# Forget-gate logits: 16 wide products with stacked weight parts, and a small product that adds the halves

## What is computed

```python
h = rmsnorm(x, norm_g[l])
proj = h @ w_in[l]
(cv_a, cv_b, cv_gate, fq, fk, fv, f_logit, fox_gate, mq, mem_gate) = jnp.split(proj, SPLITS, axis=-1)
...
logf = jax.nn.log_sigmoid(f_logit.astype(jnp.float32) + b_f[l].astype(jnp.float32))
...
cT = jnp.cumsum(logf, axis=1)
bias = ci[..., :, None] - cT[..., None, :]
```

## Time and profile before

| | us |
|---|---|
| median of 3 runs | 1780.23 (1780.03 to 1782.44) |
| the profiled execution | 1780.92 |
| its span (first to last instruction) | 1779.1 |
| PE busy | 1759.7 (99%) |
| DVE busy | 1257.5 (71%) |
| ACT busy | 942.1 (53%) |

### The profile page before, as it was taken

One profiled execution on the slowest core, in us unless ns is written; L12 is line 12 of the kernel. 1 busy time (PEld: TensorE's weight loads), 2 busy tenths in 40 slices (PEclk: granted clock), 3 DMA queues, 4 the chain that ended last, 5 costly groups with the idle time before them and its releaser, 6 DMA issues.

```text
span 1779.1 us, 29674 instructions
## 1 busy us (share of the span) xinstructions
PE 1759.7 (99%) x10231; PEld 1545.9 (87%) x10231; DVE 1257.5 (71%) x1590; ACT 942.1 (53%) x1254; POOL 616.6 (35%) x621
## 2 busy tenths in 40 slices
PE   9999999999999999999999999999999999999997
PEld 7888888888888888888888888888888888888886
DVE  6877777765598777777777644445887688887754
ACT  5544554544476555555555533334655566775532
POOL 1743345556703333111111422221252255550032
PEclk9999999999999999999999999999999999999999
DMA  8444444436565555555555555556455444444453
GB/s 315 174 160 168 167 167 176 166 142 237 189 237 189 189 189 189 189 189 189 189 189 189 168 194 184 189 194 208 166 189 201 166 166 165 165 166 165 166 189 118
DMA packets 51008, 326.61 MB, mean 184 GB/s; under 512 B 5776, under 2 KB 6416, under 8 KB 18320
## 3 DMA queue, kind: packets, MB, share of 16 engines
q1 hardware_dynamic: 49808, 323.86, 51.1%
q10 hardware_dynamic: 1152, 2.11, 0.3%
HBM read 323.85 MB, written 2.10 MB: 183 GB/s over the span
## 4 chain that ended last, share of the span: by engine, by line
PE 93%; DVE 3%; ACT 2%; DMA 1%; issue 1%; ACTq 0%; DVEq 0%; SPq 0%
PE ps L1803 57%; PE ps L1804 29%; DVE wlo L971 1%; ACT whi L466 1%; PE ps_sc L1842 1%; PE ps_lev L1928 1%; PE ps_t L1832 1%; PE ps_lev L1878 1%; DMA x_in<-in_x_turned 0%; PE ps_lev L1803 0%; DMA stage<-in_w_a 0%; PE bank_b L1933 0%; DMA stage<-in_w_b 0%; PE bank_a L1847 0%; DVE big L1408 0%
## 5 line engine op out<-in xcount | busy, mean ns | idle before, releaser
L1803 PE MATMUL ps<-act_a,whi 128*128 128x512 f32 x3056 | 1069.2, 394 | 0.0
L971 DVE TENSOR_TENSOR wlo<-stage,whi 128x2048 fp32r<-128x2048 f32 (+1 forms) x315 | 695.1, 2207 | 250.5 <-ACT whi L466 245.7
L1804 PE MATMUL ps<-act_a,wlo 128*128 128x256 f32 x3056 | 854.3, 280 | 0.0
L1803 PEld LDWEIGHTS ps<-act_a,whi 128*128 128x128 f32 x3056 | 573.7, 188 | 125.3 <-issue 0.5
L466 ACT ACTIVATE whi<-stage 128x2048 fp32r<-128x2048 f32 (+1 forms) x315 | 567.7, 1802 | 126.2 <-DMA stage<-in_w_down 103.6
L1804 PEld LDWEIGHTS ps<-act_a,wlo 128*128 128x128 f32 x3056 | 574.0, 188 | 0.3
L1803 PE MATMUL ps<-big,whi 128*128 128x512 f32 x1568 | 546.3, 393 | 3.5 <-DVE big L1408 1.3
L1804 PE MATMUL ps<-big,wlo 128*128 128x256 f32 x1568 | 438.3, 280 | 0.0
L473 ACT ACTIVATE small<-ps 128x256 f32<-128x256 f32 x242 | 92.7, 383 | 534.1 <-PE ps L1804 534.1
L1803 PEld LDWEIGHTS ps<-big,whi 128*128 128x128 f32 x1568 | 294.4, 188 | 70.1 <-DVE wlo L971 2.4
L1804 PEld LDWEIGHTS ps<-big,wlo 128*128 128x128 f32 x1568 | 294.3, 188 | 0.1
(11 more groups left out here) (373 smaller groups left out, 1340.2 us busy)
## 6 DMA issues: line engine op xcount, KB each, us to landing
stage<-in_w_a SPq DMA_DIRECT2D x166, 1024.0 KB, 4.8
stage<-in_w_b SPq DMA_DIRECT2D x87, 1024.0 KB, 4.8
stage<-in_w_down SPq DMA_DIRECT2D x64, 704.0 KB, 4.0
stage<-in_w_a SPq DMA_DIRECT2D x8, 256.0 KB, 8.6
mem_raw<-in_memT SPq DMA_DIRECT2D x1, 2048.0 KB, 9.6
mem_again<-in_memT SPq DMA_DIRECT2D x1, 2048.0 KB, 9.2
x_in<-in_x_turned ACTq DMA_DIRECT2D x7, 256.0 KB, 9.3
x_in<-in_xT SPq DMA_DIRECT2D x3, 512.0 KB, 8.9
```

Source lines behind the costliest of these rows:

```text
L971: dve.tensor_tensor(wlo[:, slot, part], stage[:, slot, part], whi[:, slot, part].bitcast(F32), ALU.subtract).then_inc(w_lo, 1)
L1803: pe.matmul(dst, whi[:, slot, c * P:(c + 1) * P], act, start=start, stop=False)
L1804: return pe.matmul(dst[:, T:2 * T], wlo[:, slot, c * P:(c + 1) * P], act[:, 0:T], start=False, stop=stop)
```

## The change

1. `wfg_hi` and `wfg_lo` become the left and right 48 columns of one tile `wfg_parts` (2048 x 96). ACT and DVE write the same numbers as before, each to its half of the columns. The tile lies elsewhere in the work area.
2. On PE, 48 products of 256 columns (3 for each of 16 feature tiles) become 16 of 512 columns with 96 stationary columns. They stand behind block 5 instead of behind block 7.
3. The result has 96 rows x 512 columns: rows of the high weight part over rows of the low part, and the activation's high part left of its low part. DVE adds the column halves (a copy from PSUM, then an add) behind `add(6)` in the conv stage's last step. It also builds `both_rows` (96 x 48, two identities over each other).
4. Behind block 7, PE waits for these (`fl_added`) and adds the row halves with one product in plain fp32, 96 rows x 256 columns, with `both_rows` as its stationary operand. That product now signals `fl_ready`. (The product of the two low parts, left out before, is in the sum now.)

```diff
-        wfg_lo = over("wfg_lo", big_at, w2[0], [P, KT, FOX_ROWS], F32R)
...
-        wfg_hi = over("wfg_hi", big_at, w2[0], [P, KT, FOX_ROWS], F32R)
+        wfg_parts = over("wfg_parts", big_at, w2[0], [P, KT, 2 * FOX_ROWS], F32R)
+        wfg_hi, wfg_lo = wfg_parts[:, :, 0:FOX_ROWS], wfg_parts[:, :, FOX_ROWS:2 * FOX_ROWS]
...
+        both_rows = work2("both_rows", [2 * FOX_ROWS, FOX_ROWS])
...
+            rows = slice(0, 2 * FOX_ROWS)
             for n in range(GROUPS):
                 u = U_CONV + 2 * n
                 add(u, 0)
+                if n == GROUPS - 1:
+                    dve.wait_ge(s("fl_parts"), 1)
+                    link(dve.tensor_tensor(both_rows[:, :], ident[rows, 0:FOX_ROWS], ident[rows, FOX_ROWS:2 * FOX_ROWS], ALU.add))
+                    link(dve.tensor_copy(fs[rows, T:2 * T], ps_t[rows, T:2 * T]))
+                    dve.tensor_tensor(fs[rows, 0:T], ps_t[rows, 0:T], fs[rows, T:2 * T], ALU.add).then_inc(s("fl_added"), 1)
...
             for j in range(2, 2 * GROUPS):
                 whole(G_CONV, 0, 0, j, U_CONV + j, j % 2, act_a)
-            pe.wait_ge(*event("wfg_ready"))
-            logits = ps_t[0:FOX_ROWS, 0:T]
-            for k in range(KT):
-                pe.matmul(logits, wfg_hi[:, k, :], act_a[:, k, 0:T], start=k == 0, stop=False)
-                pe.matmul(logits, wfg_hi[:, k, :], act_a[:, k, T:2 * T], start=False, stop=False)
-                ins = pe.matmul(logits, wfg_lo[:, k, :], act_a[:, k, 0:T], start=False, stop=k == KT - 1)
-            ins.then_inc(s("fl_ready"), 1)
+                if j == 2 * GROUPS - 3:
+                    pe.wait_ge(*event("wfg_ready"))
+                    for k in range(KT):
+                        ins = pe.matmul(ps_t[0:2 * FOX_ROWS, :], wfg_parts[:, k, :], act_a[:, k, :], start=k == 0, stop=k == KT - 1)
+                    ins.then_inc(s("fl_parts"), 1)
+            pe.wait_ge(s("fl_added"), 1)
+            pe.matmul(ps_t[0:FOX_ROWS, 0:T], both_rows[:, :], fs[0:2 * FOX_ROWS, 0:T], start=True, stop=True).then_inc(s("fl_ready"), 1)
```

More of the change, by code:

```diff
@@ L824, in _ @@
                     act.wait_ge(s("fox_in"), 3 * 16)
-                    act.activation(wfg_hi[:, :, :], wfg[:, :, :], ACT.Copy).then_inc(event("wfg_split")[0], 1)
+                    act.activation(wfg_hi, wfg[:, :, :], ACT.Copy).then_inc(event("wfg_split")[0], 1)
             act.wait_ge(*event("z_abs"))
@@ L1478, in _ @@
                     dve.wait_ge(*event("wfg_split"))
-                    dve.tensor_tensor(wfg_lo[:, :, :], wfg[:, :, :], wfg_hi[:, :, :].bitcast(F32),
+                    dve.tensor_tensor(wfg_lo, wfg[:, :, :], wfg_hi.bitcast(F32),
                                       ALU.subtract).then_inc(event("wfg_ready")[0], 1)
```

## The result

| | us |
|---|---|
| the changed kernel, median of 9 runs | 1786.56 (1784.99 to 1787.81) |
| the kernel before, median of 9 runs beside it | 1781.03 (1779.84 to 1782.44) |
| ratio, 95% interval | 1.0031 (1.0023 to 1.0040) |
| the profiled execution of the changed kernel | 1787.81, span 1786.0 |

The change makes the kernel slower, by 5.5 us (4.1 to 7.1 by the interval). The forecast was 1783.5, with a range up to 1785.5: the direction holds, the size doesn't. The profiled execution is the slowest of the nine, so lengths read from its trace lie on the long side.

The account below looks back on a forecast made before the run. PE was taken to bound the kernel, with no reserve towards DVE at block 11. From 1780.23, +1.9 (list -1.27, wait +3.3, existing loss -0.14) and +1.4 for the clock gave 1783.5 us, range 1780.6 to 1785.5.

Parts of the forecast that it names:

- PE's list: PE's own work: 5.61 us of old logits products replaced by 3.70 wide and 0.64 small, 1.27 us shorter.
- wait at block 11: PE reaches block 11 at T + 17.29 but may start only at T + 20.55, so it waits 3.3 us.
- clock: PE's clock falls to half in the wait, block 11 begins at half rate: +1.4 us, bounds 0 and 5.55.
- T: The moment when block 7 is through on PE, from which the prediction counts; 3.70 us later in the changed kernel.
- PE has no reserve at block 11: Block 11 needs DVE's `add(9)` and already lost 0.14 us; PE arriving earlier without an earlier `add(9)` must wait.
- `zf`, exp and ln holding `evac(8)`: `zf` stays at T + 5.87; `evac(8)` queues behind ACT's exp and ln until about T + 9.6.
- DVE's three instructions hidden: Between `add(6)` and `lo(9)`, DVE's new instructions take 1.0 us, covered by 1.38 us of idle time.
- no wait: Rival: PE doesn't wait at block 11 and keeps its 1.27 us, giving 1779.0 us; chance 0.06.
- Slower by over 0.2%: Rival: clock stays low through block 11's first half or longer, costing 2.8 us, total 1784.9; chance 0.23.
- the term for POOL: POOL's taps lengthening DVE's instructions before `add(9)`: bounds -0.87 (no hit) and +0.87 (a second one), taken as 0.
- the prediction's bound for one hit: By the strict port rule, a DVE instruction could lose a whole POOL instruction at once, 2.96 us.
- the chain from T to `evac(8)`: From block 7's end through `zf`, exp and ln, ACT frees `evac(8)` at about T + 9.6, 1.76 sooner than before.

Follow-up runs that it names:

- pool_late: The changed kernel with POOL's first convolution taps held until DVE has made `cpos` and `cneg`; 1782.44 us, 1.0010 against the kernel before.
- moved_only: The kernel before with its 48 old logits products only moved from behind block 7 to behind block 5; 1788.25 us, ratio 1.0045 against the kernel before.
- act_first: The changed kernel with ACT's `evac(8)` and `hi(11)` moved ahead of the forget gate's exp and ln; 1779.89 us, 0.9994 against the kernel before.
- act_first_pool_late: The changed kernel with ACT's `evac(8)` and `hi(11)` ahead of exp and ln, and POOL's first taps held until `cpos` and `cneg`; 1779.20 us, ratio 0.9993.
- keep_clock: The changed kernel with 18 small dummy products on PE between block 10 and block 11; 1785.11 us, 1.0021 against the kernel before.

## Why the prediction was wrong

Per term, from the changed kernel's trace:

| term | forecast | measured |
|---|---|---|
| wide products | 3.70 | 3.74 |
| small product | 0.64 | 0.76 |
| PE's list | -1.27 | -1.11 |
| wait at block 11 | +3.3, less the 0.14 of before | +5.6, less 0.05 |
| clock | +1.4 | +1.6 |
| sum | +3.3 | +6.06 |

Measured: the small product's 0.76 is the second pair of block 8 (1396.74) less T less a pair's 0.35; it includes 0.1 more than the column sums, which I leave unexplained. The wait is block 11's start, 1418.65, less what PE alone would make, T + 0.76 + 16.65 = 1413.04; the 0.05 is how late block 11 started before. The clock's term is 7.33 - 5.73 (before: 1418.76 - 1413.03). Of the 2.3 by which the wait is longer than forecast, POOL makes 2.04 and the later `evac(8)` 0.45, less 0.12 for the dearer small product.

Part of the miss in the median, 3.06 us, isn't the change's: the sum starts from 1780.23, the median of three runs, and the nine runs beside the changed kernel have 1781.03. That is 0.8.

**What held.** The reading that PE has no reserve at block 11; `zf`, exp and ln holding `evac(8)`; DVE's three instructions hidden; the wait there, put down to DVE; the clock falling in it, in all nine executions as their mean clocks say (0.996 or 0.997, against 0.998 in the execution before). The "no wait" rival is out by the trace. "Slower by over 0.2%" came true (5.5 us against 3.56), but not by a clock that stays low: that needed over 1.66 us, and the clock cost 1.6. A further hit by POOL, which it named only beside that, is what decided.

**What failed: the term for POOL.** I bounded it by -0.87 and +0.87 and took 0. It measured +2.04 (10.22 against 8.18). I had seen one of DVE's instructions hit beside POOL's first add and allowed one more like it. I had not worked out which instructions would lie beside which of POOL's adds. The trace of before had all that was needed. ACT waited there for PE twice, 1.75 us ahead of `evac(8)` and 1.39 us ahead of `evac(9)`:

```profile
1407.63 0.38 ACT L473 ACTIVATE small<-ps 128x256 f32<-128x256 f32 x1 [1.39 <-PE ps L1804]
```

In the sum I used the first of these waits only. The second goes too, and with it ACT's products for POOL, and POOL's adds, come 1.5 us earlier against the gate: from the start of `lo(11)` to POOL's first add it was 1410.68 - 1404.30 = 6.38 us, now it is 1412.77 - 1407.88 = 4.89. So the gate's last instructions run into three adds and not one. Three of these records are longer than before: 0.89 (1.24 - 0.35), 0.90 (1.89 - 0.99), and 0.24 for `cpos` (1.51 - 1.27, it was hit before too). That makes 2.03. pool_late showed it by taking all of it away.

The rule of the Trainium skill that I weighed and left at the edge ("SBUF — State Buffer", the section on the two separate sides: a lock for a whole instruction, which goes to the one that starts first) was the better guide. `cc` at L1510 starts at 1413.14, while POOL's first add is under way (to 1414.23); it ends at 1414.38. The first of the pair at L1512 meets the second add (to 1415.50) and ends at 1415.79, `cpos` meets the third (to 1417.70) and ends at 1417.85. Each ends 0.15 to 0.29 us behind the add. The other way round, POOL's fourth add starts at 1417.65, when `cneg`, `add(9)` and `lo(12)` run at their usual lengths, and lasts 7.41: there POOL is the one that waits. One thing doesn't fit by the records: `cpos` starts 0.09 us ahead of the third add and waits it out all the same; whether starts so close are in their true order isn't shown.

With the adds taken singly, the prediction's bound for one hit was misread too. It took half of a row of two, 2.96 us. In the kernel before, these two last 1.40 and 4.55: the first hit `cpos`, the second is long because POOL itself waited. A hit costs 0.9 to 1.1 us here, and the question was how many there would be.

**A second, smaller miss:** the chain from T to `evac(8)` was 10.06 instead of 9.6. ACT's `hi(10)` waited 0.42 us for its weights to land (row at 1396.63), and `zf` came at T + 6.41 instead of 5.87. In pool_late and moved_only this wait isn't there, in act_first it is 0.32, in act_first_pool_late 0.54. So it differs between kernels that have the same wide products. None of the three traces with the old 48 products has it; with one trace for each kernel it stays open whether the change makes it likelier. It passes straight into PE's wait, since the chain has no reserve.

**The range** ended at 1785.5, for it paired a clock cost of 2.8 with no loss from POOL, and the clock's 1.4 with at most one more hit. The two unknowns add up; with +2.0 for POOL the sum of the prediction gives 1785.5, with the late weights 1786.0, inside the spread of the nine runs. From the base of 1781.03 it would be 1786.8 against 1786.56.

## What to carry to other kernels

An engine at 99% doesn't say that its list is all that counts: look for the block at which it arrives just as its partner is done. If it is made faster ahead of that point, ask which links of the partner's chain move along; here a stretch of 5.6 us of PE work had been the cover for exp, ln and their queue on ACT. Where the next chain runs beside other engines, lay both lists beside each other at the new times before bounding contention, instruction by instruction; and count an idle of PE of 2 us at more than its length.

## What the runs showed of the hardware

- PE's granted clock fell after a wait of 2.03 us (pool_late, the profiled execution; by the mean clocks in seven of ten), and only when work was back: the wait ended at 1413.64, the products slowed at 1415.14 and were fast again at 1418.34. So a stretch at 1.2 GHz needn't lie in the gap that caused it, nor right behind it. In the changed kernel the fall came in the gap at 1415.3, and full clock was back at about 1422.2. The cost was much the same both times: five pairs at 0.64 instead of 0.35, some 1.5 us (in the changed kernel the first of them took 0.78).
- A wait of 0.97 us behind 4.2 us of dummy products left the clock at full (keep_clock).
- A DVE instruction of 0.35 us took 1.24, one of 0.48 took 1.38, one of 0.41 (`cpos`) took 1.51, when it met one of POOL's 512-column adds. Such an add took 1.27 to 1.46 us where it held up DVE, and 4.55 (before) and 7.41 (changed) where it started beside `cneg` and DVE's long subtractions followed.
